# Moving the weight slots and the constants of a float32r encoder layer to the top of SBUF

## The reference, cut to what matters

```python
cond = jax.nn.silu(c)
mod = cond @ w_ada + b_ada                      # six vectors of 2048: shift, scale, gate, twice
hn = modulated_rms_norm(h, sh1, sc1)
proj = hn @ w_in                                # 2048 -> 5664 columns
attn_out = axial_gqa_attention(...)             # 8 query heads, 2 kv heads of 128
dn_out = bidir_gated_deltanet(...)              # 8 heads, both directions, chunked delta rule
h = h + gt1 * (concat([attn_out, dn_out]) @ w_out)
hn = modulated_rms_norm(h, sh2, sc2)
u = dwconv_centred(hn @ w_up, w_ffn_conv) + b_ffn_conv      # 2048 -> 2 x 5632
h = h + gt2 * ((silu(u_gate) * u_val) @ w_down)             # 5632 -> 2048
return rms_norm(h) * final_norm
```

## The kernel before, in words

| tensor | before | after the change |
|---|---|---|
| `act_hi` (32,768 bytes) | 16,512 | 16,512 |
| `x_feat`, `otok`, `act_lo` (32,768) | 49,280 | 49,280 |
| `raw` 0 and 1 (4,096 each) | 82,048 | 191,744 |
| `w_hi` 0 and 1 | 90,240 | 199,936 |
| `w_lo` 0 and 1 | 98,432 | 208,128 |
| `cst` | 106,624 | 216,320 |
| `wba_hi`, `ka`, `mh_hi`, `xs` (start of the shared region) | 118,112 | 82,048 |
| `mh_lo` | 140,640 | 104,576 |
| `T` of the mixer | 205,952 | 169,888 |

## Time and profile before

### The profile page before, as it was taken

One profiled execution on the slowest core, in us unless ns is written; L12 is line 12 of the kernel. 1 busy time (PEld: TensorE's weight loads), 2 busy tenths in 40 slices (PEclk: granted clock), 3 DMA queues, 4 the chain that ended last, 5 costly groups with the idle time before them and its releaser, 6 DMA issues.

```text
span 2720.8 us, 35447 instructions
## 1 busy us (share of the span) xinstructions
PE 2576.9 (95%) x12198; PEld 2096.4 (77%) x12198; DVE 1431.9 (53%) x1846; ACT 1018.0 (37%) x1422; POOL 189.4 (7%) x270
## 2 busy tenths in 40 slices
PE   2589999999999989988999999999999999999997
PEld 2467888888888868776888888887888888888885
DVE  5835666666666653446444444444344444444454
ACT  4124344344344343334443234442234432223334
POOL 2200211211211201100000000000000000000000
PEclk9689999999999989999999999999999999999998
DMA  9935445444444422432333333333333323333233
GB/s 339 307 98 161 139 117 148 139 118 145 139 120 142 139 62 63 132 93 62 97 96 90 92 104 93 100 91 90 105 93 97 96 87 95 103 98 95 86 91 124
DMA packets 436095, 318.42 MB, mean 117 GB/s; under 512 B 12582, under 2 KB 408657, under 8 KB 435537
## 3 DMA queue, kind: packets, MB, share of 16 engines
q1 hardware_dynamic: 406192, 212.19, 27.3%
q0 software_dynamic: 28928, 104.87, 12.1%
q10 hardware_dynamic: 929, 0.74, 0.1%
HBM read 313.56 MB, written 4.19 MB: 117 GB/s over the span
## 4 chain that ended last, share of the span: by engine, by line
PE 89%; DVE 4%; DMA 3%; issue 2%; ACT 1%; ACTq 0%; DVEq 0%
PE pw L1307 23%; PE pw L1309 23%; PE pw L1308 23%; PE pw L1291 2%; PE pw L1293 2%; PE pw L1292 2%; PE pd L1523 2%; PE pd L1546 1%; PE pd L1559 1%; DMA T<-in_w_ada_dram 1%; PE pd L1506 1%; PE pd L1566 1%; DMA DD<-in_w_ada_dram 1%; DVE ada_acc L864 1%; DVE PTb L864 1%
## 5 line engine op out<-in xcount | busy, mean ns | idle before, releaser
L1307 PE MATMUL pw<-act_hi,w_hi 128*128 128x512 f32 x2048 | 825.8, 403 | 12.9 <-DVE act_lo L1202 9.2
L848 DVE TENSOR_TENSOR w_lo<-raw,w_hi 128x1024 fp32r<-128x1024 f32 x426 | 520.6, 1222 | 548.9 <-ACT w_hi L502 546.4
L1309 PE MATMUL pw<-act_hi,w_lo 128*128 128x512 f32 x2048 | 800.4, 391 | 0.0
L1308 PE MATMUL pw<-act_lo,w_hi 128*128 128x512 f32 x2048 | 798.7, 390 | 0.0
L502 ACT ACTIVATE w_hi<-raw 128x1024 fp32r<-128x1024 f32 x426 | 450.2, 1057 | 518.9 <-PE pw L1309 433.2
L1307 PEld LDWEIGHTS pw<-act_hi,w_hi 128*128 128x128 f32 x2048 | 385.6, 188 | 108.0 <-issue 23.3
L1309 PEld LDWEIGHTS pw<-act_hi,w_lo 128*128 128x128 f32 x2048 | 385.2, 188 | 82.8
L1308 PEld LDWEIGHTS pw<-act_lo,w_hi 128*128 128x128 f32 x2048 | 385.9, 188 | 81.9 <-issue 7.2
L1307 PE MATMUL pw<-mh_hi,w_hi 128*128 128x512 f32 x704 | 280.4, 398 | 1.1 <-DVE w_lo L848 1.1
L1308 PE MATMUL pw<-mh_lo,w_hi 128*128 128x512 f32 x704 | 278.3, 395 | 0.0
L1309 PE MATMUL pw<-mh_hi,w_lo 128*128 128x512 f32 x704 | 278.3, 395 | 0.0
(11 more groups left out here) (264 smaller groups left out, 2555.3 us busy)
## 6 DMA issues: line engine op xcount, KB each, us to landing
raw<-in_w_up_dram SPq DMA_DIRECT2D x176, 512.0 KB, 4.1
ada_w<-in_w_ada_dram POOLq DMA_DIRECT2D x128, 512.0 KB, 4.3
raw<-in_w_in_dram SPq DMA_DIRECT2D x88, 512.0 KB, 3.8
raw<-in_w_down_dram SPq DMA_DIRECT2D x64, 384.0 KB, 3.5
raw<-in_w_down_dram SPq DMA_DIRECT2D x64, 320.0 KB, 3.2
raw<-in_w_out_dram SPq DMA_DIRECT2D x32, 512.0 KB, 4.4
DD<-in_w_ada_dram POOLq DMA_DIRECT2D x16, 512.0 KB, 5.5
EG<-in_w_ada_dram POOLq DMA_DIRECT2D x16, 512.0 KB, 5.2
```

Of the source, the lines that this page charges most:

```text
L848: V.tensor_tensor(w_lo[slot][:], raw[slot][:], w_hi[slot][:].bitcast(F32), ALU.subtract).then_inc(lo_made.sem, 1)
L1307: M(bank, w_hi[slot][:, k, :], hi[:, k0 + k, :], start=first, stop=False)
L1308: M(bank, w_hi[slot][:, k, :], lo[:, k0 + k, :], start=False, stop=False)
L1309: ins = M(bank, w_lo[slot][:, k, :], hi[:, k0 + k, :], start=False, stop=last)
```

## The change

Only the placing in SBUF changes; no instruction is added, taken away or moved. The weight slots, the constants and the small vectors are allocated last instead of before the shared region. A tensor `reserved` of 109,696 bytes, which nothing uses, stands in for the shared region (the mixer's tensors need the most, 109,688 bytes), and the moved tensors lie above it. `xs` becomes a member of the shared region in form; its place relative to the region's start stays.

```diff
+REGION = 109696
...
         act_lo = sb("act_lo", [P, KT, S], F32R)
-        raw = [sb(f"raw{i}", [P, UK, P]) for i in range(2)]
-        w_hi = [sb(f"w_hi{i}", [P, UK, P], F32R) for i in range(2)]
-        w_lo = [sb(f"w_lo{i}", [P, UK, P], F32R) for i in range(2)]
-        cst = sb("cst_sb", [P, C_N])
-        col = sb("col", [P, V_N])
-        mod = sb("mod", [P, 6 * KT])
-        cond = sb("cond", [P, KT])
-        nrm = sb("nrm", [P, 3, NB])
...
         mlp.close()
         X_SLOTS = 4
-        xs = ctx.enter_context(nc.sbuf_tensor("xs", [P, X_SLOTS, NB, P], F32))
+        rows_of_x = ExitStack()
+        xs = sb("xs", [P, X_SLOTS, NB, P], F32, rows_of_x)
+        rows_of_x.close()
+        sb("reserved", [P, REGION // 4], F32)
+        raw = [sb(f"raw{i}", [P, UK, P]) for i in range(2)]
+        w_hi = [sb(f"w_hi{i}", [P, UK, P], F32R) for i in range(2)]
+        w_lo = [sb(f"w_lo{i}", [P, UK, P], F32R) for i in range(2)]
+        cst = sb("cst_sb", [P, C_N])
+        col = sb("col", [P, V_N])
+        mod = sb("mod", [P, 6 * KT])
+        cond = sb("cond", [P, KT])
+        nrm = sb("nrm", [P, 3, NB])
```

## The result

The change makes the kernel slower: 2755.42 us (2753.93 to 2757.73, 4 runs) against 2724.15 us, a ratio of 1.0115 with a 95% interval of 1.0098 to 1.0133. The forecast was 2709.6 us, with a range from 2702 to 2730 for the first three cases; the second rival had 2761.

A forecast was written before the change was run, and what follows sets the result against it. TensorE, busy 95% of the span, was taken to bound the kernel through its matmul rate. 2723.7 us less 14.1 from `down`, all other terms 0, gave 2709.6; own range 2706 to 2713, wider range 2702 to 2730.

The forecast's parts named there:

- the first three cases: Forecast 2709.6 us, 0.52; mixer gain besides, 2702.8, 0.06; `down` staying slow, 2723.7 (2729.5 with the transposes), 0.22.
- the second rival: `up`, output projection and stream slow to 233.33 ns by the new distance, 37.6 us; `down` gains nothing; 2761 us, chance 0.20.
- the one on `up` and the projections: 7,104 matmuls with `act_*` moving were taken to stay at 226.67 ns although their distance from the weights changes.
- the pieces in the mixer: 23 stream pieces in 8 heads, about 8 slow matmuls each after float32 work: 6.8 us to win back, none taken.
- order and 64-byte alignment: In `down`, `mh_*` lay above the weights and 32 bytes past a 64-byte boundary; both put right, 226.67 ns was expected.
- evidence in the gate projection: Its 48 matmuls take 229.0 ns each, going between two rates as the weights move by 128 modulo 256.
- the distances seen: Modulo 256: 0 and -32 fast, 32 in `down` and 96 in the gate projection slow, 128 not seen.
- The term of `down`: 2112 matmuls of `down` on the path go from 233.33 to 226.67 ns, a gain of 14.1 us.
- Transposes and other engines at 0: 872 transposes cost nothing (5.8 us kept for the range); better-aligned VectorE, ScalarE and DMA tiles gain 0, hidden under TensorE.
- The rule of the skill: TensorE's two independent read ports never wait, so no placing could change a matmul's rate; the result would be 2723.7 us.

The follow-up runs named there:

- the series: Kernels without the layer: series of 72 matmuls, each with its own distance between weights and moving tiles; float32r at 226.66 ns (distance 0) to 234.3 ns (96).
- the kernel with the larger reserve: Changed kernel with 384 bytes more of reserve, weights a multiple of 512 bytes above every moving tile: 2708.67 us against 2723.29, ratio 0.9946.
- the table: Float32r rates without the layer by distance modulo 256: 226.66 ns at 0, 232.4 at 128, 228.9 at 192, 234.3 at 96, 233.3 at 32, 64, 160, 224.

## Why the prediction was wrong

The reading of what bounds the kernel held: same instructions, TensorE alone changed, and its rate set the end. The step that failed is the one on `up` and the projections, "I take 226.67, but this is the weak place". It costs 232.4 - 226.67 = 5.73 ns a matmul: 5630 x 5.73 = 32.3 us, less 2112 x 0.93 = 2.0 us of `down`, gives 30.3; measured were 31.3. That the two agree within 1 us is in part luck, as smaller terms that the sum leaves out cancel: the matmuls behind a switch, which the 5630 leave out, lost too (see the pieces in the mixer), the first `up` grew by 4.1 us and not by 6.0, and most of the 3.3 us up to the end of the gate projection isn't the rate.

*Why `down` was slow.* The prediction named order and 64-byte alignment, and took their both being met as two reasons for one forecast. Neither is a reason. The distance was 32 modulo 256, and a pad of 32 bytes takes `down` to 120.6 us, with the order unchanged. An expectation that rests on two explanations that were never told apart isn't twice as safe, if a third fits the same rows.

*The rival that came true.* It had the mechanism: the change moves the weights by 128 modulo 256 against `act_*`. It had its evidence in the gate projection, and it listed the distances seen. One of them doesn't hold beyond that stretch: -32, which is 224 modulo 256, passed as fast, and with 128 columns of weights it has 233.3 ns. I gave it 0.20, because everything was on 64-byte boundaries; the series say that this counts for nothing. Its size, 37.6 us and 2761, was too high by a term: distance 128 has 232.4 ns and not 233.33, so 32.3 us instead of 37.6, and `down` does win its 0.9 ns.

*The term of `down`.* Where the distance is 0 the gain is 123.85 - 120.6 = 3.3 us in each of the first three chunks and 2.7 in the fourth, 12.5 us in all, against the 14.1 that I wrote. A part of what is missing stands at the weights of its second unit, which TensorE reaches earlier: in the first `down` it waits 0.35 us there in the kernel with the larger reserve, 0.23 before.

*Transposes and other engines at 0.* Right: 272 ns before and after, and VectorE busy 1432.1 us against 1431.9. Float32 showed no dependence at the three distances tried.

*Pieces in the mixer.* I said that a new distance could win back up to 6.8 us after the switches, and took none. By start times from 225 to 1170 us, before has 782 intervals over 229 ns among 1980, 5.2 us over the rate of 226.67 in all. With the larger reserve it is 634 and 4.1 us, with 32 bytes of pad 623 and 4.0 us. So 1 us was there. It didn't come from the distance of weights and moving tiles, which the pad leaves as it was in these pieces, but from where the shared region lies, with the float32 operands used just before them; the pad moves nothing else. After the change the same stretch has 1463 intervals over 229 ns among 1940 and 11.1 us over the rate. In the 161 pieces of six matmuls and more, the up to eight intervals that follow the first one went from 230.7 to 232.3 ns on average, 1.7 us in all. The prediction, and its second rival too, took these matmuls to be slow already and so past slowing.

*The rule of the skill.* The Trainium skill, "SBUF — State Buffer", section "Who interferes with whom", has TensorE wait on no one through its two read ports. For bfloat16 and float32 the series agree: 215.83 and 429.17 ns at every distance. For float32r they don't: 226.7 to 234.3 ns in the table, by the place of the two operands alone.

*What stays open.* Why the rate follows this distance with a period of 256 bytes, whether the weight load and the moving read get in each other's way or something else is at work, and why not in bfloat16 or float32, isn't shown. Nor does the table explain the gate projection: with 32 columns of weights at a constant distance the series have 230.5 to 233.3 ns and never 226.67, which that stretch had in four of six intervals. Its distance changes from block to block, 224 and 96 by turns, and so does its rate. After the change it has 0 and 128 by turns, and its 48 matmuls take 11.16 us, 232.5 ns each. A rule for that isn't in these runs.

## What to carry to other kernels

In a kernel of float32r matmuls with 512 columns moved, a fresh weight load for each and 128 columns of weights, put weights and moving tiles at a distance that is a multiple of 256 bytes, and let both step by such multiples (a step of 32 bytes more in both cost 3.5 ns although each pair stayed at distance 0); tensors rounded up to 32 bytes end up there by luck only, and any small tensor added ahead of them can cost or give 0.4 to 2%. Read the rate from starts, long stretch by long stretch: two stretches with the same shapes and different rates ask for a list of their addresses. Before blaming what an address looks like (high, low, aligned), list everything that the fast and slow stretches differ in, and try a pad of 32 bytes.

## What the runs showed of the hardware that was not expected

- Float32r, 512 columns, 128 columns of weights loaded for each matmul: 226.66 ns at distance 0 modulo 256 and 228.9 to 234.3 ns at the seven other multiples of 32; absolute place and order don't enter. This holds where both step by multiples of 256 bytes; the distances 240 and 252 have 226.66 too.
- Bfloat16 in the same pattern has 215.83 ns, so even the best float32r placing is 10.8 ns slower for a matmul. Why is open.
- After a switch from float32 to float32r work the first eight or so matmuls run at 230 to 231 ns on average before the rate of their distance is reached, at distance 0 too; the place of the float32 operands has a say in how many. In the series, which have no such switch, a rate of 226.66 ns was reached within the first 24 every time.
